# State-space inputs turned through a DRAM scratch, and 512-column gate and up products in ten turns

## What is computed

```python
for layer in range(DEPTH):
    h = h + 0.5 * swiglu_ffn(rms_norm(h, ffn1_norm[layer]), ffn1_w_in[layer], ffn1_w_out[layer])
    hn = rms_norm(h, mix_norm[layer])
    ...   # layer 0: s5_mixer, layer 1: stick_breaking_mixer
    h = h + mixed
    h = h + 0.5 * swiglu_ffn(rms_norm(h, ffn2_norm[layer]), ffn2_w_in[layer], ffn2_w_out[layer])
def swiglu_ffn(h, w_in, w_out):
    gate, up = jnp.split(h @ w_in, 2, axis=-1)
    return (jax.nn.silu(gate) * up) @ w_out
```

## Time and profile before

| | us |
|---|---|
| median of 3 runs | 1001.94 |
| lowest, highest | 1001.79, 1002.18 |
| span of the profiled execution, first to last instruction | 999.6 |
| median less span (launch and end) | 2.3 |
| PE busy, DVE busy, ACT busy, POOL busy in the span | 987.1, 744.5, 571.2, 114.4 |
| granted TensorE clock, mean over the span | 0.999 |

### The profile page before, as it was taken

One profiled execution on the slowest core, in us unless ns is written; L12 is line 12 of the kernel. 1 busy time (PEld: TensorE's weight loads), 2 busy tenths in 40 slices (PEclk: granted clock), 3 DMA queues, 4 the chain that ended last, 5 costly groups with the idle time before them and its releaser, 6 DMA issues.

```text
span 999.6 us, 19015 instructions
## 1 busy us (share of the span) xinstructions
PE 987.1 (99%) x7304; PEld 904.0 (90%) x7304; DVE 744.5 (74%) x922; ACT 571.2 (57%) x794; POOL 114.4 (11%) x144
## 2 busy tenths in 40 slices
PE   8999999999999999999999999999999999999997
PEld 8999999989999888888898888888899898888886
DVE  5789986889976777777687777776566587666666
ACT  7444447573365655555465555555599765555555
POOL 4854138100001000000010000001000010000000
PEclk9999999999999999999999999999999999999999
DMA  7555555443075565666646666566544256655563
GB/s 253 192 174 183 170 177 164 149 132 121 23 218 184 183 196 185 190 183 191 196 148 214 189 188 190 184 180 193 186 126 125 85 154 218 190 192 188 190 190 108
DMA packets 49049, 172.57 MB, mean 173 GB/s; under 512 B 6097, under 2 KB 6097, under 8 KB 48977
## 3 DMA queue, kind: packets, MB, share of 16 engines
q1 hardware_dynamic: 48544, 170.99, 54.3%
q10 hardware_dynamic: 432, 0.55, 0.2%
HBM read 170.47 MB, written 1.05 MB: 172 GB/s over the span
## 4 chain that ended last, share of the span: by engine, by line
PE 73%; DVE 13%; POOL 6%; ACT 4%; issue 4%; DMA 1%; SPq 0%; DVEq 0%; POOLq 0%; ACTq 0%
PE mx L1314 11%; PE gu L1314 11%; PE mx L1317 6%; PE gu L1317 6%; PE acc L1356 4%; PE gu L1299 4%; PE gu L1300 4%; PE gu L1301 4%; DVE w_lo L803 4%; PE acc L1360 2%; PE gu L1356 2%; PE mx L1356 2%; PE acc L1343 2%; PE acc L1345 2%; PE acc L1347 2%
## 5 line engine op out<-in xcount | busy, mean ns | idle before, releaser
L803 DVE TENSOR_TENSOR w_lo<-raw,w_hi 128x1024 fp32r<-128x1024 f32 x258 | 324.3, 1266 | 91.0 <-ACT w_hi L364 90.4
L364 ACT ACTIVATE w_hi<-raw 128x1024 fp32r<-128x1024 f32 x259 | 270.5, 1052 | 80.8 <-DMA raw<-wstream_dram 22.3
L1299 PE MATMUL gu<-g,w_hi 128*128 128x256 f32 x560 | 161.4, 288 | 1.5 <-DVE g L943 1.3
L1300 PE MATMUL gu<-g,w_hi 128*128 128x256 f32 x560 | 158.4, 283 | 0.0
L1301 PE MATMUL gu<-g,w_lo 128*128 128x256 f32 x560 | 158.4, 283 | 0.0
L1314 PE MATMUL mx<-g,w_hi 128*128 128x512 f32 x480 | 119.9, 392 | 0.0
L1314 PE MATMUL gu<-g,w_hi 128*128 128x512 f32 x464 | 116.2, 392 | 0.0
L1299 PEld LDWEIGHTS gu<-g,w_hi 128*128 128x128 f32 x560 | 107.3, 192 | 2.3 <-issue 1.5
L1300 PEld LDWEIGHTS gu<-g,w_hi 128*128 128x128 f32 x560 | 107.4, 192 | 0.1
L1301 PEld LDWEIGHTS gu<-g,w_lo 128*128 128x128 f32 x560 | 107.3, 192 | 0.0
L1314 PEld LDWEIGHTS mx<-g,w_hi 128*128 128x128 f32 x480 | 87.0, 189 | 16.0
(11 more groups left out here) (309 smaller groups left out, 1927.1 us busy)
## 6 DMA issues: line engine op xcount, KB each, us to landing
raw<-wstream_dram SPq DMA_DIRECT2D x318, 512.0 KB, 3.7
x<-x_in_dram SPq DMA_DIRECT2D x4, 256.0 KB, 5.9
raw<-wstream_dram SPq DMA_DIRECT2D x3, 256.0 KB, 5.7
out_dram<-x_tok SPq DMA_DIRECT2D x3, 256.0 KB, 2.0
gain_row<-last_gain_dram SPq DMA_DIRECT2D x1, 512.0 KB, 4.4
raw<-wstream_dram ACTq DMA_DIRECT2D x1, 256.0 KB, 4.6
...
```

The source lines that it names most:

```text
L364: act.activation(weights(unit)[0], raw[:, s_raw, :], ACT.Copy).then_inc(hi_ready, 1)
L803: dve.tensor_tensor(lo, raw[:, n % RAW, :], hi.bitcast(F32), ALU.subtract).then_inc(lo_ready, 1)
L1299: pe.matmul(dst, a, hi, start=start, stop=False, skip_group_check=check)
L1300: pe.matmul(dst, a, lo, start=False, stop=False, skip_group_check=check)
```

## The change

The b operand of the state-space inputs arrives a second time, already turned on the host (`b_turned`). PE turns only the small table of powers (two transposes in turn 5), ACT copies it out, SP writes it to a DRAM scratch and reads it back, each row to 16 partitions (four writes after unit 24, two reads of 16x2048 after each of units 25 to 32; `b_turned` comes in eight reads of 32x2048 after every second unit from 9 to 23). DVE's products of turns 9 to 14 are made in the turned layout. The padding copies go from POOL to ACT (`pad_out`, `pad_in`, `pad_zero`, `pad_now`), POOL makes the product of the current step alone (`s5_now`), and rotations come a turn earlier. Turns 6 to 12 and 18 to 20 run `wide_unit`, with `mx` in even and `gu` in odd turns. In the diff a line of "..." stands for what is left out.

```diff
+POWERS_TURNED, POWERS_STORED, POWERS_READ, INPUTS_READ = 5, 24, range(25, 33), range(9, 25, 2)
+OUT_PAD_TURNS, NOW_TURN = (6, 7, 9, 10), 14
+IN_PADS = {17: ((0,), (1,)), 18: ((2,), (3, 4)), 19: ((), (5,)), 20: ((6,), (7,))}
...
-FIRST_PRODUCT, FIRST_TURNED, KERNEL_TURN, LATE_TURNED, FIRST_ROTATED = 3, 7, 15, 18, 17
+FIRST_PRODUCT, KERNEL_TURN, FIRST_ROTATED, DECAY_TURN = 3, 15, 16, 19
+WIDE_FIRST = (*range(6, 13), 18, 19, 20)
...
+        in_t = [arena[:, 16384 + 2048 * r:18432 + 2048 * r] for r in range(2)]
+        powers_t = [arena[:, 20480 + 2048 * r:22528 + 2048 * r] for r in range(2)]
+        in_now = low[:, 0:2048].rearrange("p (r a c) -> p r a c", r=2, a=PAIRS)
+        spare = low[:, 2048:4096]
...
-            turns = UNITS // RAW
-            with sp.Fori(2, turns) as i:
+            def store_powers():
+                sp.wait_ge(powers_copied, 1)
+                for k in range(2):
+                    for g2 in range(2):
+                        sp.dma_start(powers_dram[g2, 2 * k:2 * k + 2].rearrange("j r a p -> (j r a) p"),
+                                     powers_rows[:, P * k + STATE * g2:P * k + STATE * (g2 + 1)]).then_inc(
+                            powers_stored, 16)
+            def read_powers(r, j):
+                if r == 0 and j == 0:
+                    sp.wait_ge(powers_stored, 16 * 4)
+                for g2 in range(2):
+                    first = CH * j + GROUP * g2
+                    sp.dma_start(powers_t[r][first:first + GROUP, :],
+                                 powers_dram[g2, j, r:r + 1].rearrange("r a p -> r (a p)").broadcast_to(
+                                     [GROUP, PAIRS * STATE])).then_inc(powers_loaded, 16)
+            def read_inputs(r, j):
+                sp.dma_start(in_t[r][CH * j:CH * (j + 1), :], b_turned[r]).then_inc(inputs_loaded, 16)
+            turns, spread = UNITS // RAW, POWERS_READ[-1] // RAW + 1
+            for unit in range(2 * RAW, RAW * spread):
+                load(unit, slot(RAW, unit), unit - RAW + 1)
+                if unit in INPUTS_READ:
+                    read_inputs(*divmod(INPUTS_READ.index(unit), STEPS))
...
+                if unit == POWERS_STORED:
+                    store_powers()
+                if unit in POWERS_READ:
+                    read_powers(*divmod(POWERS_READ.index(unit), STEPS))
+            with sp.Fori(spread, turns) as i:
                 for s in range(RAW):
                     load(RAW * i + s, s, RAW * i + (s - RAW + 1))
...
-            def read_turned(k):
-                act.wait_ge(turned, k + 1)
-                act.activation(*turned_state(k), ACT.Copy).then_inc(turned_read, 1)
+            def read_powers():
+                act.wait_ge(powers_turned, 1)
+                act.activation(powers_rows, mx[:, 0, 0:2 * P], ACT.Copy).then_inc(powers_copied, 1)
...
+            def pad_out(k):
+                r, g2, half = k // 4, k // 2 % 2, k % 2
+                act.wait_ge(dense_ready, r + 1)
+                act.wait_ge(out_cleared, 1)
+                rows, cols = group_half(g2)
+                pairs = slice(PAIRS // 2 * half, PAIRS // 2 * (half + 1))
+                dst = state_out.rearrange("p r a (j c) -> p r a j c", j=STEPS)
+                act.activation(dst[rows, r, pairs, :, cols], dense[r][rows, pairs], ACT.Copy).then_inc(padded, 1)
...
+            def pad_in(k):
+                r, g2, half = k // 4, k // 2 % 2, k % 2
+                if k == 0:
+                    act.wait_ge(in_dense_ready, 2)
+                    act.wait_ge(mask_ready, 2)
+                    act.wait_ge(kernels_done, 2)
+                elif k == 4:
+                    act.wait_ge(powers_stored, 16 * 4)
+                    act.wait_ge(rot_half, 1)
+                src = powers_t[r].rearrange("p (a s) -> p a s", a=PAIRS)
+                pairs = slice(PAIRS // 2 * half, PAIRS // 2 * (half + 1))
+                act.activation(state_in[r][:, pairs, STATE * g2:STATE * (g2 + 1)], src[:, pairs, :], ACT.Copy,
+                               scale=group_mask[:, g2:g2 + 1]).then_inc(in_padded, 1)
...
+                if f in (3, 4) and not late:
+                    pad_zero(f - 3)
+                if f in OUT_PAD_TURNS:
+                    k = 4 * (OUT_PAD_TURNS.index(f) // 2) + 2 * (OUT_PAD_TURNS.index(f) % 2) + late
+                    pad_out(k)
+                if f == NOW_TURN and late or f == NOW_TURN + 1 and not late:
+                    pad_now(f - NOW_TURN)
+                for k in IN_PADS.get(f, ((), ()))[late]:
+                    pad_in(k)
...
                 split_after(g0)
-                if 0 <= early < 8:
-                    read_turned(early)
-                if 8 <= late < 16:
-                    read_turned(late)
-                if late == 12:
+                if f == POWERS_TURNED:
+                    read_powers()
+                prep_copies(f, 0)
+                if f == DECAY_TURN:
                     act.wait_ge(rot_started, 1)
+                    act.wait_ge(in_padded, 4)
                     act.activation(rho[:, :, 1:CHUNKS], par[:, 19, :].unsqueeze(2).broadcast_to(
                         [P, PAIRS, CHUNKS - 1]), ACT.Copy).then_inc(decay_ready, 1)
                 if KERNEL_TURN < f <= KERNEL_TURN + 2:
                     read_kernels(f - KERNEL_TURN - 1, range(0, 2))
+                if f in WIDE_FIRST:
+                    act.wait_ge(unit_done, g0 + 2)
+                    act.wait_ge(hlo_ready, f - 1)
+                    act.activation(tmp[:, f % 2, 2:4, :], (mx, gu)[f % 2][:, :, SEQ:2 * SEQ],
+                                   ACT.Copy).then_inc(low_copied, 1)
                 silu(0, f)
                 split_after(g0 + 1)
                 round_h(0, f)
                 if KERNEL_TURN < f <= KERNEL_TURN + 2:
                     read_kernels(f - KERNEL_TURN - 1, range(2, 3))
-                if 0 <= early < 8:
-                    read_turned(early + 1)
-                if 8 <= late < 16:
-                    read_turned(late + 1)
+                prep_copies(f, 1)
...
+            def in_product(k):
+                real = dense[0].rearrange("p a j h -> p (a j h)")
+                if k == 0:
+                    dve.wait_ge(inputs_loaded, 16 * 2 * STEPS)
+                    dve.wait_ge(powers_loaded, 16 * 2 * STEPS)
+                    dve.wait_ge(padded, 4)
+                    dve.tensor_tensor(real, powers_t[0], in_t[0], ALU.mult)
+                elif k == 1:
+                    dve.wait_ge(powers_loaded, 16 * 4 * STEPS)
+                    dve.tensor_tensor(spare, powers_t[1], in_t[1], ALU.mult)
+                elif k == 2:
+                    step(dve.tensor_tensor(powers_t[0], powers_t[0], in_t[1], ALU.mult))
+                elif k == 3:
+                    step(dve.tensor_tensor(powers_t[1], powers_t[1], in_t[0], ALU.mult))
+                elif k == 4:
+                    dve.tensor_tensor(powers_t[1], powers_t[1], powers_t[0], ALU.add).then_inc(in_dense_ready, 1)
+                else:
+                    dve.wait_ge(in_dense_ready, 1)
+                    dve.tensor_tensor(powers_t[0], real, spare, ALU.subtract).then_inc(in_dense_ready, 1)
...
-                if 0 <= f - FIRST_PRODUCT < 12:
-                    s5_product(f - FIRST_PRODUCT)
-                scale_gu(f % 2, g0 + 2)
+                if 0 <= f - FIRST_PRODUCT < 6:
+                    out_product(f - FIRST_PRODUCT)
+                elif 6 <= f - FIRST_PRODUCT < 12:
+                    in_product(f - FIRST_PRODUCT - 6)
+                if f in WIDE_FIRST:
+                    sum_gu(f % 2, WIDE_FIRST.index(f) + 1, f + 1)
+                else:
+                    scale_gu(f % 2, g0 + 2)
...
                 if 0 <= f - FIRST_ROTATED < 4:
                     if f == FIRST_ROTATED:
                         dve.wait_ge(rot_started, 1)
+                    if f == FIRST_ROTATED + 2:
+                        dve.wait_ge(kernels_done, 2)
                     s5_rotation(SMALL_ROTATIONS + (f - FIRST_ROTATED) // 2, (f - FIRST_ROTATED) % 2)
+                    if f == FIRST_ROTATED + 1:
+                        dve.sem_inc(rot_half, 1)
                     if f == FIRST_ROTATED + 3:
                         dve.sem_inc(rot_ready, 1)
...
-            def turn(k):
-                if k == 0:
-                    pe.wait_ge(const_ready, 1)
-                    pe.wait_ge(padded, 2)
-                elif k == 8:
-                    pe.wait_ge(padded, 4)
-                    pe.wait_ge(toep_act, 2)
-                    pe.wait_ge(toep_dve, 1)
-                elif k == 9:
-                    pe.wait_ge(toep_act, 4)
-                    pe.wait_ge(toep_dve, 2)
-                if k >= 2:
-                    pe.wait_ge(turned_read, k - 1)
-                for a in range(4):
-                    mm = pe.transpose(mx[:, k % 2, P * a:P * (a + 1)], b_pow[:, k // 8, 4 * (k % 8) + a, :],
-                                      ident[:, :])
-                mm.then_inc(turned, 1)
```

(66 more changed lines are left out.)

105 lines of the change are left out of this document (67 added, 38 removed).

## The result

The changed kernel takes 1021.53 us (median of 6 runs, 1018.75 to 1025.99), the kernel before beside it 1002.06: ratio 1.0195, 95% interval 1.0175 to 1.0216. The forecast was 1005.0 with a range to 1010. The sign was right; the size was a sixth of it. The profiled execution has a span of 1019.0 us against 999.6, so its 19.4 us stand for the difference.

The account below looks back on a forecast made before the run. The prediction took PE to set the pace, with DVE close behind. Its -8.5 us and the losses summed to +3.1 on the 999.6 span, 1002.7; with the median's 2.3 that gave 1005.0, range 995 to 1010.

Parts of the forecast that it names:

- -8.5 us on PE: PE: 16 transpose groups gone (6.9 us), twenty units with 512-column matmuls save 1.8, two new transposes cost 0.2.
- Transfers, 0: DMA stream: two small reads behind a unit make 2.4 us, under PE's 2.85, so no loss.
- Rival B: Powers reads into 16 partitions are slow and make ACT's splits wait in turns 9 to 11; 1007 to 1011, chance 0.17.
- the sum: All terms added: +3.1 us, giving 1005.0; its case, 1004 to 1008, had chance 0.33.
- `s5_now`, +0.5 (0 to 1.7): Turns 9 to 12: six products still on POOL slow one of DVE's splits, +0.5 us.
- Wide turns, +3.15 before their gain: Turns 6 to 12: DVE's turn grows to 8.91 us against PE's 8.46, losing 0.45 in each of seven.
- Pads, +2.6: Turns 6, 7, 9, 10: of ACT's second 1.05 us padding copy 0.65 comes through, four times.
- Powers late, +0.8: Turn 3: `s5_negate` on POOL delays DVE's first product by 2.24 us, of which 1.45 is covered by lead.
- Gate 18, +3.5: Turn 18: PE's gate unit writes `mx`, so waits for ACT's last kernel copies of turn 17; +3.5 us.
- End, +1.0: End of the feed-forward: PE waits 1.04 us for DVE already, and +1.0 us more (0 to 1.8).

Follow-up runs that it names:

- e10: e7 also without GpSimd's six current-step products, so neither powers reads nor those products; 1000.49 us (0.9980).
- e5: e2 with the current step's operand padded a turn earlier (turns 13 and 14); 1006.53 us (1.0062).
- e4: Changed kernel with 512-column products in turns 6 to 12 alone, 256 columns in turns 18 to 20; 1013.85 us (1.0107).
- e2: Changed kernel with 256-column gate and up products in all turns of the first feed-forward; 1008.96 us (1.0074).
- e11: e10 with the eight output padding copies cut to one sixteenth of their columns; 997.59 us (0.9958).
- e7: e5 without the sixteen reads of the powers and SP's wait for their stores, GpSimd writing zeros instead; 1004.13 us (1.0018).
- e1: Changed kernel with powers read back in eight 512-column transfers over 128 partitions instead of sixteen of 2048 columns over 16; 1021.75 us (1.0195).
- e15: e5 with e1's reads over 128 partitions, stored by eight plain writes, two behind each of units 21 to 24; 1008.27 us (1.0066).
- e16: e9 with the 128-partition reads and eight plain writes of e15; 1004.42 us (1.0019).
- e9: e5 without GpSimd's six current-step products, two memsets standing for them; 1005.82 us (1.0035).
- e13: e10 with 512-column products in turns 6 to 12 again; 1004.08 us (1.0017).
- e8: e2 with the four padding copies of turns 9 and 10 moved to turns 12 and 13; 1009.90 us (1.0071).
- e12: e6 with GpSimd's six products released when VectorE has scaled gate and up, not at `hlo_ready`; 1010.42 us (1.0082).
- e6: e5 with powers stored after unit 20, one read behind each of units 21 to 36, the inputs' second and third products exchanged; 1007.22 us (1.0054).

## Why the forecast was wrong, term by term

The forecast was 16.4 us too low, and no single term makes that. In the order in which the edits took them off, the parts above their forecast are: the reads and GpSimd's products 5.5 (6.0 for 0.5, e10 against e5), turns 18 to 20 3.7 (7.7 for 3.5 + 1.0 - 0.5, e4), turns 6 to 12 3.0 (4.9 for 1.9, e2 against e4), `pad_now` 2.4 (e5), the rotation turns 2.3 (what e11 keeps), the pads 0.3; and 0.8 for late powers did not come. The first is the largest, and 2.4 to 5.3 us of it (by the order in which the two are taken off) is a term that the prediction put at nothing.

**-8.5 us on PE: right as work taken away, not as time.** L1551 is gone, and wide units follow each other by 2.80 us (103.44 to 106.24 in PE's timeline after). With the wide turns, the reads, GpSimd's products and most of the output pads taken off, e11 is 4.3 us below the kernel before it, of the 6.7 that the transposes were to give.

**Transfers, 0: the step that failed.** The prediction argued that "by bytes 0.8 us: 2.4 per unit, under the 2.85 that PE needs". That asks whether the engines can carry the bytes on average. What counts is how long one unit takes from its issue to its landing, because SP issues unit n only when unit n-3 is split: 3.7 to 4.6 us before, 7.0 in this window after, 9.83 for the unit of turn 9. ScalarE waited 7.2 us for the stream in four places; the first of them, 1.6 us at 68, comes before any read of the powers, beside the reads of `b_turned`, and stays in e7. Rival B gave the right symptom, splits that wait for the stream (at 90, 98 and 102 us, for units of turns 9 and 10; it said 9 to 11), and the right sign, but its mechanism (partitions) was only half right, and its 1007 to 1011 is as far off as the sum. The Trainium skill ("SBUF — State Buffer", section "Door 1: The DMA port swizzle") says that 16 partitions reach four of 16 ports. The engines' share per byte agrees in kind: 1.54 times that of the earlier trace rows with the narrow reads, and 0.81/253 = 1.02 times with e1's. But undoing it gained nothing in e1 and e15 and at most 1.4 us in e16, so this occupation was not the main thing that PE waited for. Leaving the reads out was worth 2.4 us (e7) to 5.3 (e10 against e9).

**`s5_now`, +0.5 (0 to 1.7): mis-sized.** Its release by `hlo_ready` puts each product on VectorE's splits: 4.5 us on VectorE, 3.6 in the time (e10 against e7), 0.7 while the reads hide it.

**Wide turns, +3.15 before their gain: the wait right, mis-sized.** Net of 1.3 us gained, the forecast had +1.9 for turns 6 to 12; alone they measured +3.6 (e13), in company +4.9 (e4 against e2), in which the clock behind three pauses of e4 is contained.

**Pads, +2.6: the number near (2.9, e11), the way wrong, so the nearness is luck.** They were to come through in turns 6 to 10. There PE felt 0.6 us of them; the rest came through GpSimd's tables in the turns from 18 on, a way that the prediction did not follow.

**Powers late, +0.8: nothing.** The first product starts at 42.92 without a wait for GpSimd (its powers are done at 42.06), and turn 4's down unit doesn't wait. The lead there was 0.3 us (48.81 to 49.15), so it was close: in e8 that unit waits 0.43.

**`pad_now`, not priced: +3.8 in its turns, +2.4 in the time (e5).** The second copy stood behind a pair of splits on ScalarE, and PE's kernels of turn 15 wait for it. ScalarE's timeline:

```profile
158.03 2.00 ACT L411 ACTIVATE w_hi<-raw 128x1024 fp32r<-128x1024 f32 x2
159.94 1.26 ACT L631 ACTIVATE low_part<-s_memory 64x512 f32<-64x512 f32 x2
```

It ends at 161.20, and PE goes on at 161.46. The prediction named `pad_in` and `pad_out` and overlooked this one, an added wait like gate 18's.

**Gate 18, +3.5: the wait right (4.3), its price not.** Turns 18 to 20 cost 7.7 us, where 4.0 was forecast with the end. Behind the wait the clock was at its lower level, which is 2.8 us of that. In turns 9 and 15 it cost 1.5 and 1.3 us: each of the three pauses that the clock followed cost about one and a half times its length. The prediction had no term for the clock.

**End, +1.0: measured 1.36 - 1.04 = +0.3.** But a part of the transposes' 3.4 us in turns 18 to 21 was never to be had: in e5, with 256 columns and no transposes, VectorE scales at 188.96 and at 198.49, 9.5 us apart, as in the earlier trace rows, and PE waits 0.5 to 1.0 us in each of turns 18 to 21 for `w_lo`. The prediction had the 9.51 beside PE's 8.64 and charged it to the wide turns alone.

Summed in medians: changed 1021.5, without wide turns 18 to 20 1013.9, without 6 to 12 1009.0, `pad_now` earlier 1006.5, no reads and no products on GpSimd 1000.5, no output pads 997.6; the remaining distance to 1002 - 6.7 = 995.3 is 2.3. That the rotation turns hold it is argued from PE's 2.1 us of waits there in e11. The edits test GpSimd's tables only in the other direction: e12 made them later and lost 3.2 us; no version releases them earlier. The steps depend on their order, as e7, e9 and e10 show. Left open: what in SP's queue makes a unit late when the engines have a fifth of their time free (e15). No version here that computes everything is faster than the kernel before; the best two, e5 and e6, take 1.0062 and 1.0054 of its time.
